# One level of the HGRN2 scores, of four positions, from exponentials of summed logs in place of products of gates

## What is computed

```python
f = lower_bound + (1.0 - lower_bound) * jax.nn.sigmoid(f_logit)
log_f = jnp.log(f)
k = 1.0 - f
...
b = jnp.cumsum(gb, axis=-2)                      # gb: log_f of a chunk
diff = b[:, :, :, None, :] - b[:, :, None, :, :]
decay = jnp.exp(jnp.where(causal[:, :, None], diff, -jnp.inf))
scores = jnp.einsum('bhtk,bhsk,bhtsk->bhts', qb, kb, decay)
o = (jnp.einsum('bhts,bhsv->bhtv', scores, ib)
     + jnp.einsum('bhtk,bhkv->bhtv', qb * jnp.exp(b), state))
```

## Time and profile before

| what | value |
|---|---|
| median of 3 runs | 1377.9 us (1377.32 to 1381.92) |
| profiled execution | 1383.02 us, of which the span of the trace is 1381.2 us |
| TensorE busy | 1235.4 us, 89% of the span |
| VectorE, ScalarE, GpSimd busy | 510.2, 327.0, 99.7 us |
| the HGRN2 loop | about 449 to 495 us of the span |

### The profile page before, as it was taken

One profiled execution on the slowest core, in us unless ns is written; L12 is line 12 of the kernel. 1 busy time (PEld: TensorE's weight loads), 2 busy tenths in 40 slices (PEclk: granted clock), 3 DMA queues, 4 the chain that ended last, 5 costly groups with the idle time before them and its releaser, 6 DMA issues.

```text
span 1381.2 us, 18645 instructions
## 1 busy us (share of the span) xinstructions
PE 1235.4 (89%) x7606; PEld 623.7 (45%) x7606; DVE 510.2 (37%) x1039; ACT 327.0 (24%) x811; POOL 99.7 (7%) x176
## 2 busy tenths in 40 slices
PE   8999888888999888888789998888889999888885
PEld 7465634333444645343324665343334465433432
DVE  1486311012784984111118554111117676211103
ACT  1232322121323623221212103221212351222211
POOL 2222000000000610000000000000002040000000
PEclk9999999999999999999999999999999999999998
DMA  9856999999934349999999959999999348999995
GB/s 316 338 197 252 366 423 428 427 427 425 404 142 181 126 169 419 426 428 426 428 426 407 389 183 359 424 428 427 428 427 401 142 183 342 364 428 428 427 428 232
DMA packets 38026, 484.20 MB, mean 351 GB/s; under 512 B 4592, under 2 KB 4928, under 8 KB 7600
## 3 DMA queue, kind: packets, MB, share of 16 engines
q1 hardware_dynamic: 36000, 478.11, 84.2%
q0 software_dynamic: 1792, 4.32, 1.1%
q10 hardware_dynamic: 144, 0.47, 0.1%
HBM read 481.77 MB, written 1.05 MB: 350 GB/s over the span
## 4 chain that ended last, share of the span: by engine, by line
PE 69%; DMA 17%; DVE 7%; ACT 3%; issue 2%; POOL 1%; DVEq 0%; SPq 0%; ACTq 0%; POOLq 0%
PE psum L925 17%; PE psum L1267 12%; DMA ring<-in_units 10%; PE psum L1201 8%; PE psum L951 7%; DMA memory<-in_units 7%; PE psum L1309 6%; PE psum L1301 6%; PE psum L894 4%; ACT memory L1438 2%; PE psum L857 2%; PE psum L1394 1%; DVE memory L2318 1%; ACT memory L1681 1%; PE psum L1071 1%
## 5 line engine op out<-in xcount | busy, mean ns | idle before, releaser
L925 PE MATMUL psum<-ring,memory 128*128 128x512 f32 x440 | 192.9, 594 | 2.4 <-DVE ring L1935 1.7
L1201 PE MATMUL psum<-memory,x 128*128 128x128 f32 x1024 | 130.5, 281 | 35.8 <-ACT memory L1438 35.0
L1309 PE MATMUL psum<-memory 128*128 128x512 f32 x240 | 119.0, 618 | 42.9 <-DVE memory L2318 22.8
L1267 PE MATMUL psum<-ring,memory 128*32 128x512 f32 x1192 | 137.2, 594 | 17.8 <-DMA ring<-in_units 12.9
L1438 ACT ACTIVATE memory<-psum,affine_t 128x128 f32<-128x128 f32 x312 | 117.6, 458 | 144.7 <-PE psum L1201 137.7
L1201 PEld LDWEIGHTS psum<-memory,x 128*128 128x128 f32 x1024 | 119.1, 191 | 71.8 <-issue 67.7
L2313 DVE TENSOR_TENSOR memory<-memory,psum 128x256 f32<-128x256 f32 x32 | 13.5, 421 | 349.4 <-ACT memory L1669 349.4
L925 PEld LDWEIGHTS psum<-ring,memory 128*128 128x128 f32 x440 | 82.7, 190 | 104.6 <-issue 103.7
L1434 ACT ACTIVATE memory<-psum 128x512 f32<-128x512 f32 (+2 forms) x105 | 54.4, 540 | 233.1 <-PE psum L925 196.3
L1267 PE MATMUL psum<-memory 128*32 128x512 f32 x856 | 98.0, 595 | 2.3 <-ACT memory L1438 1.6
L1309 PEld LDWEIGHTS psum<-memory 128*128 128x128 f32 x240 | 40.6, 189 | 124.1 <-DVE memory L2318 48.6
(11 more groups left out here) (248 smaller groups left out, 1384.0 us busy)
## 6 DMA issues: line engine op xcount, KB each, us to landing
ring<-in_units SPq DMA_DIRECT2D x126, 2048.0 KB, 26.0
memory<-in_units SPq DMA_DIRECT2D x87, 2048.0 KB, 22.6
memory<-in_units SPq DMA_DIRECT2D x21, 1024.0 KB, 11.3
ring<-in_units SPq DMA_DIRECT2D x3, 1024.0 KB, 7.0
ring<-in_units SPq DMA_DIRECT2D x4, 512.0 KB, 7.6
memory<-in_ln_ffn_g POOLq DMA_DIRECT2D x3, 512.0 KB, 11.9
memory<-in_ln_ffn_b POOLq DMA_DIRECT2D x3, 512.0 KB, 17.5
memory<-in_const SPq DMA_DIRECT2D x3, 456.0 KB, 34.5
```

What stands on the lines that cost most here:

```text
L925: last = nc.tensor.matmul(bank(key), tokens[:, k, :], weights[:, k, :], start=(k == 0 and p not in (6, 7, 3)), stop=(k == KD // 2 - 1), sk ...
L1201: last = nc.tensor.matmul(psum[:, to, (at + i) * P:(at + i + 1) * P], x[:, c, k * P:(k + 1) * P], sel[:, par, c, :], start=(c == 0), stop= ...
L1267: last = nc.tensor.matmul(psum[rows, 0, :].rearrange("p (t f) -> p t f", t=2), xw[:, k, rows], wk[:, e], start=(k == 0), stop=(k == KD - 1))
L1309: last = nc.tensor.matmul(psum[:, 4 + NH * c + h, :], hT[:, FC + c, :], y_sb[:, h * HB:(h + 1) * HB], start=False, stop=last_quad, skip_gr ...
```

## The change

SUMMED becomes 5: the level of four joins the levels whose decays are exponentials of summed logs. `within` grows from 192 to 256 columns, so that each matmul of L1110 has 256 columns and each of the first two Exps writes 512 elements a partition in place of 384. The loops over `LEVELS[:SUMMED]` run five times. The products of gates for the level of four fall away on VectorE (L2124, L2126 and, ahead of the loop, L2091 to L2093), on GpSimd (L817, L818) and the second key copy on ScalarE, and with them the semaphores products_made and two_ready. `qk` keeps its eight entries in another order; CROSS stays right behind the summed levels, which makes it entry 5. The tables in DRAM grow from 1088 to 1152 columns.

```diff
-SUMMED = 4
-CROSS, FOUR, TWO, ONE, NL = SUMMED, SUMMED + 1, SUMMED + 2, SUMMED + 3, SUMMED + 4
+SUMMED = 5
+FOUR, CROSS, TWO, ONE, NL = SUMMED - 1, SUMMED, SUMMED + 1, SUMMED + 2, SUMMED + 3
...
-                        step(nc.gpsimd.tensor_tensor(e[:, :, :, 0], fours(k)[:, :, :, 0], fours(f)[:, :, :, 1], ALU.mult))
-                        if h == 0:
-
-                            pool.wait_ge(products_made, 2)
-                        pool.wait_ge(keys_copied, 2 * (h + 1))
-                        eights = lambda t: t.rearrange("p c (b r) -> p c b r", r=8)
-                        two, four = eights(qk[:, h % 2, :, TWO, :]), eights(qk[:, h % 2, :, FOUR, :])
-                        by = g23[:, h].rearrange("p (c b) -> p c b", c=TC).unsqueeze(3).to_broadcast([P, TC, P // 8, 2])
-                        nc.gpsimd.tensor_tensor(four[:, :, :, 0:2], two[:, :, :, 0:2], by, ALU.mult)
-                        nc.gpsimd.tensor_tensor(four[:, :, :, 2], eights(k)[:, :, :, 2], eights(f)[:, :, :, 3], ALU.mult)
+                        nc.gpsimd.tensor_tensor(e[:, :, :, 0], fours(k)[:, :, :, 0], fours(f)[:, :, :, 1], ALU.mult)
+                        pool.wait_ge(keys_copied, h + 1)
...
-                        for i, r in ((TWO, 4), (FOUR, 8)):
-                            runs = lambda t: t.rearrange("p c (b r) -> p c b r", r=r)[:, :, :, r // 2 - 1]
-                            k = kT[:, h, :].rearrange("p (c t) -> p c t", c=TC)
-                            nc.scalar.activation(runs(qk[:, h % 2, :, i, :]), runs(k), ACT.Copy).then_inc(keys_copied, 1)
+                        second = lambda t: t.rearrange("p c (b r) -> p c b r", r=4)[:, :, :, 1]
+                        k = kT[:, h, :].rearrange("p (c t) -> p c t", c=TC)
+                        nc.scalar.activation(second(qk[:, h % 2, :, TWO, :]), second(k), ACT.Copy).then_inc(keys_copied, 1)
...
-                gate = fT.rearrange("p h (b r) -> p h b r", r=8)
-                v.tensor_copy(g45[:, :, :, 0], gate[:, :, :, 4])
-                v.tensor_tensor(g45[:, :, :, 1], gate[:, :, :, 4], gate[:, :, :, 5], ALU.mult).then_inc(products_made, 1)
-                v.tensor_tensor(g23, gate[:, :, :, 2], gate[:, :, :, 3], ALU.mult).then_inc(products_made, 1)
...
-                        v.tensor_tensor(fours(two)[:, :, :, 3], fours(one)[:, :, :, 3], fours(f)[:, :, :, 2], ALU.mult).then_inc(two_ready, 1)
-                        if h == 0:
-
-                            dve.wait_ge(products_made, 2)
-                        eights = lambda t: t.rearrange("p c (b r) -> p c b r", r=8)
-                        four, by = qk[:, h % 2, :, FOUR, :], g45[:, h].rearrange("p (c b) r -> p c b r", c=TC)
-                        v.tensor_tensor(eights(four)[:, :, :, 4:6], eights(q)[:, :, :, 4:6], by, ALU.mult)
-                        dve.wait_ge(two_ready, h + 1)
-                        v.tensor_tensor(eights(four)[:, :, :, 6:8], eights(two)[:, :, :, 6:8],
-                                        by[:, :, :, 1:2].to_broadcast([P, TC, P // 8, 2]), ALU.mult)
+                        v.tensor_tensor(fours(two)[:, :, :, 3], fours(one)[:, :, :, 3], fours(f)[:, :, :, 2], ALU.mult)
```

More of the change, by code:

```diff
@@ L400, in build @@
         hgrn_sums = region(extra, 7168, [4, KD // 2, P])
-        g45 = region(work, O_AT, [HH, T // 8, 2])
-        g23 = region(work, O_AT + 512, [HH, T // 8])
         heads_out = region(memory, 0, [TC, D])
@@ L517, in build @@
         odd_ready, level_picked = sem("odd_ready"), sem("level_picked")
-        products_made, two_ready = sem("products_made"), sem("two_ready")
         pad_set, z_made = sem("pad_set"), sem("z_made")
```

## The result

The changed kernel takes 1383.37 us (median of 20 runs, 1380.01 to 1387.88), the kernel before 1379.04 us beside it (20 runs, 1376.69 to 1382.38). The ratio is 1.0029, with a 95% interval of 1.0021 to 1.0037: a small loss of some 4 us, just under what was named as the bound of no change. The forecast had the sign right and the size wrong, +1.5 us, and 1383.37 lies 0.4 above its range. 1.1 us of the miss are the median of before, which was 1377.9 from three runs and 1379.04 from twenty. The rest, some 2.8 us, is the subject here. Two later sets of runs gave 1.0027 (1.0013 to 1.0040) and 1.0033 (1.0019 to 1.0047).

The account below looks back on a forecast made before the run. The prediction took VectorE's instructions to bound each round. Rounds 1.3, round 0 0.47 and later Exps 0.21 made 2.0 us, less 0.54 for escaped collisions: +1.5 us, 1379.4 against a median of 1377.9, range 1374.0 to 1383.0.

Parts of the forecast that it names:

- What bounds the loop: HGRN2 layer's loop: a round lasts as long as VectorE's instructions take; VectorE is busy 29.67 of 30.70 us.
- The price of a collision: In the loop, each GpSimd product that runs beside VectorE's products takes 0.27 us from VectorE.
- Rival B: In the loop, GpSimd blocks VectorE for its whole instruction, 0.46 us in place of 0.27: +3.5 us, 1381.4; chance 0.08.
- The own work: VectorE per round: two gate products out, one query product in, -0.28 + 0.20 = -0.08 us.
- the start: Round 0: one more query product and collision, +0.47 us, and Exps ending later without cover, +0.21 us.
- the discount of 0.54 us: Over the loop: two of eight added GpSimd products meet no VectorE product, lowering the sum from 2.0 to +1.5 us.
- six collisions become seven: Each round: one more GpSimd product beside VectorE's, +0.27 us, with VectorE's -0.08 making +0.19, +1.3 for rounds 1 to 7.
- The step on the log sums: TensorE's wider log sums end the Exps some 0.2 us later: hidden in steady rounds, +0.21 us in round 0.
- Rival A: In the loop, VectorE's removed gate products go at full price, collisions included: -3.9 us, 1374.0; chance 0.15.
- Rival C: In the loop, all nine VectorE products collide and take 4.2 us: +7.4 us, 1385.3; chance 0.12.
- Rival D: In the rounds, saved work, dropped waits and added collision cancel, leaving 0 to +0.7 us from round 0: 1378.3; chance 0.17.
- the change outside the loop: Sign against the forecast: its base is wrong if the time changes outside the HGRN2 layer's loop.

Follow-up runs that it names:

- a_keys_on_vector: The changed kernel with all key products moved from GpSimd to VectorE: rounds of 4.94 us, ratio 0.9995 to the kernel before.
- b_keys_vector: The kernel before with all key products moved from GpSimd to VectorE, ahead of its last query product: rounds of 4.81 us, ratio 0.9986.
- b_wide_sums: The kernel before with log sums of 256 columns, of which the Exps read the first 192: rounds of 5.30 us, ratio 1.0010.
- a_two: The changed kernel with two key products on VectorE, the other four on GpSimd behind VectorE's last query product: ratio 1.0000 to the kernel before.
- b_pool_behind: The kernel before with GpSimd's key products waiting for VectorE's last query product of the same head: rounds of 4.69 us, ratio 1.0010.
- a_filler: The changed kernel with filler matmuls where TensorE waits at the loop's end: rounds of 5.43 us, ratio 1.0022 to the kernel before.
- a_key4_out: The changed kernel without GpSimd's key product of the level of four: rounds of 5.13 us; its ratio of 0.9999 isn't used.

## Why the prediction was right or wrong

**What bounds the loop** held: VectorE is full before and after (29.67 and 29.74 of 30.70 us), and the chain runs over its lines.

**The price of a collision** held: 0.27 us forecast, 0.47 against 0.20 us for a product in the changed kernel's rows, and 0.29 and 0.30 a round by the added and the removed product. Rival B, with 0.46 for the whole instruction and 0.38 a round, is refuted by the same numbers. The Trainium skill has it (SBUF — State Buffer, section SBUF: two separate sides) that the loser is blocked for the whole instruction. A chain of such products doesn't pay that here: a GpSimd product lasts 0.46 us and costs 0.27.

**The own work**, -0.28 + 0.20, held (with the key product's 0.20 it makes 0.12, and a_keys_on_vector lies 0.13 over b_keys_vector). So did the start: +0.47, +0.21 and one round's 0.19 are 0.87, and the first mask pick came 0.88 us later, of which 0.21 are there at the first query product.

**The step that failed first is the discount of 0.54 us**, "I let two of the eight added collisions escape". None did, on balance. Over the six rounds behind the first mask pick a round grows by 0.26 us while VectorE's own work falls by 0.08; the 0.34 between them are 7.5 prices of 0.27 us in six rounds, where six were counted. Without the discount the sum was 2.0, against 2.4 in the loop.

**The step below it is the count "six collisions become seven", +0.19 us a round, where 0.26 was measured.** It was read from one round, and a short one. In that round the first of GpSimd's six costs 0.1 us and not 0.27. In the four middle rounds the change adds 0.23 us on average, near the forecast. It adds 0.16 in the last and 0.48 in the first of the six (4.71 to 5.19), where two more products collide.

**The step on the log sums failed in its reasoning.** "In steady rounds this is hidden" was argued from 1.2 us of slack before VectorE would wait. It never waits there, and b_wide_sums still lost 0.13 us a round: the Exps also release GpSimd, and a shift of 0.2 us of GpSimd's block is enough to put one more of its products beside VectorE's in the short rounds. The parts aren't additive, though. The TensorE part alone costs +0.13, the collision +0.27 to 0.29 and the own work -0.08; together that would be 0.32 to 0.34, and the change costs 0.26.

**Rival A** fell for the reason given against it: the removed products' full price didn't go with them, it passed to the next instruction in the row. **Rival C** fell too: two of the nine products still run at 0.20 us, and the nine take 3.56, not 4.2. **Rival D** fell with rounds 0.26 us longer.

**What the sum left out**: 0.6 us outside the span, the change outside the loop that the prediction named as a sign against its base. It doesn't follow the change alone, since a_keys_on_vector and a_two, which contain it, lie at 1.85. No run shows its cause.

**What stays open**: the runs of the changed kernel have a span 3.5 us longer than those of before (1380.93 +- 0.31 against 1377.40 +- 0.18 us, standard errors, 42 and 119 runs), the loop gives 2.4, and the remaining 1.1 us isn't placed. With the 0.6 us outside the span, then, some 1.7 of the 4.1 us of loss have no cause that a run shows. The drop of the clock at the loop's end, 1.4 us where it comes, would fit in size; the mean clocks and the filler don't confirm it. The profiles don't place it behind the loop either: from the output projection on, the two of before take 885.5 and 881.3 us, the three of the changed kernel 883.2, 882.6 and 881.5.

## What to carry to other kernels

Where the instructions of a second engine lengthen those of a full one, moving work to the second may cost the first more than doing it itself: here some 0.27 us against 0.20. Count the instructions of the second engine that lie beside those of the full one, not its busy time, and put them beside instructions that don't compete, which took a round from 5.17 to 4.50 us. Look at several rounds, not one: here they differed by 0.2 us in turn, and the one that was read had fewer collisions than its neighbours. And slack against a wait is not slack against a collision: what starts a second engine 0.2 us later can cost, though nobody waits for it.

## What the runs showed of the hardware that was not expected

- A product of VectorE with both operands in SBUF and 128 elements a partition takes 0.20 us from start to start alone and 0.42 to 0.49 beside a GpSimd product, 0.46 or 0.47 in the middle of a row of them. With 64 elements it takes 0.13 to 0.19 alone and 0.41 to 0.46 beside one. The output product, which reads one operand from PSUM, is unmoved: 0.41 us beside GpSimd (L2144 in the earlier trace rows) and with GpSimd idle (L2119 at 483.79 after the change, where L806 ends at 483.32).
- The granted clock fell to its lower level for 3.4 to 10.2 us within or behind the loop in most profiles, each time after a stretch in which TensorE waited about half the time or more (b_pool_behind: busy 1.06 of the 3.3 us ahead of the first drop, 1.35 of 3.4 ahead of the second). It did not fall after every such stretch, as the two profiles at the end of the changed kernel's loop show.
- The changed kernel (all three sets) and a_filler had 2.4 to 2.5 us outside the span on average, a_key4_out 2.16, and the other kernels of the table whose time is used 1.83 to 1.87 us.
